# Context attention moved to other steps of an expert layer, two activations moved behind a copy, attention maxima taken negated

## The chip, the cores and the metric

One core of a Trainium2 chip runs the whole program. The metric is the device time in microseconds (us) of one execution, median over the runs. All arithmetic is in float32.

## What is computed

The reference has two blocks with a width of 1024 and a sequence of 256 tokens. Two parts of it matter here. The first is the mixture of experts that ends block one, the second is the attention of block two, on a context of 256 tokens (layer 0 only gives it an output) and on the latent tokens (both layers).

```python
# expert_choice_moe: 16 experts, each takes 32 of the 256 tokens
hid = jax.nn.silu(jnp.einsum('becd,edf->becf', xs, w_gate)) * jnp.einsum('becd,edf->becf', xs, w_up)
y = jnp.einsum('becf,efd->becd', hid, w_down) * g[..., None].astype(xn.dtype)

# block two, per head of 64
q_ga_c = rms_norm_2(to_heads(ga_qc, GQA_Q_HEADS), q_norm_w)
def context_attention(q, k, v):
    s = jnp.einsum('bgrqd,bgkd->bgrqk', q, k) * (q.shape[-1] ** -0.5)
    p = jax.nn.softmax(s, axis=-1).astype(v.dtype)
    return jnp.einsum('bgrqk,bgkd->bgrqd', p, v)

# layer 1 of the context only gives a state and keys
w = jnp.exp(b[:, :, -1:, :] - b)                 # key decays
return jnp.einsum('bhsd,bhsv->bhdv', k * w, v)
```

The context does not depend on block one, so its work can be done while block one still runs.

## The kernel before

Each engine runs one instruction list, in the order in which the program writes it, and waits on semaphores. All large weights come over SyncE's queue in one fixed order (`stream`) into a ring in SBUF of 4 x 4096 columns, that is four tiles of 2 MB (L3168 and L3166 issue them). A tile is issued when TensorE has finished with the tile whose place it takes (`freed`).

The mixture of experts is a list of 96 steps, `STEPS`: four groups of 16 steps "gate" and "up" (two halves for each of 4 experts) and 8 steps "down". Steps 16 to 23, 40 to 47, 64 to 71 and 88 to 95 are down steps. Every step reads two tiles of 2 MB: L1653 is the gate and up product (32 matmul records a tile), L1679 the down product (16 records a tile). At the head of a new expert, and of the first down step, TensorE turns the hidden tokens (L1667, `turn_hidden`), ScalarE copies them (L1916, `by_feature`), and the down product waits for that copy. After the last down step of a group VectorE copies the result out (L2273, L2274), and in the next four gate steps TensorE combines it into the tokens (L1692, `combine`) and VectorE adds it (L2251). In every second up step ScalarE takes the silu of the hidden values (L1912).

The context work is cut into 80 stages, `CTX_STAGES`, and `CTX_AT` says behind which step each stands. A stage is a piece of a generator on TensorE, ScalarE and VectorE alike (`context()`), run after the engine's own work of that step. Its weights, 0.5 to 1 MB, stand in the stream behind the step's tiles. The stages `lv0` to `lv2` (L844, with GpSimd's L3113 and VectorE's L2747 to L2754), `gla_out` (L863), `gla_norm` and `at0` to `at5` read no weights. Each of `at0` to `at5` does two heads: scores (L937), largest value (L2914, L2915), exponential (L2500), normalising (L2920, L2921), turning (L945), copy (L2301), values (L955), where one head's path goes over three engines.

Stage `gqa_kv1`, behind step 87, projects keys and values of context layer 1; ScalarE then evacuates them (L2301), squares the keys (L2360) and takes the key decays (L2386), all before it returns to the copy of step 88 (L1916).

The latent attention of each layer has 24 units of 128 queries and 512 keys. VectorE takes a unit's maximum (`largest`, L3012) and multiplies it by -1 or -0.125 (L3013), ScalarE uses it as the bias of the exponential (L2596), VectorE inverts the sum (L3018), GpSimd multiplies (L3123), TensorE turns.

## Time and profile before

| what | value |
|---|---|
| median of 3 runs | 2214.92 us (2212.74 to 2216.28) |
| the profiled execution's own time | 2211.93 us |
| its span | 2210.1 us |
| TensorE matmul busy | 1981.3 us, 90% |
| VectorE, ScalarE, GpSimd busy | 599.8, 423.2, 207.2 us |
| mean granted TensorE clock | 0.966 of full |
| HBM read | 661.08 MB |

The span begins with the first instruction. The expert steps fill about 301 to 1359 us of it, the latent layers what follows. A busy share is a mean over stages with different limits, and matmul busy time contains time in which the array ran at half clock, so 90% does not say that TensorE sets the time everywhere. The rows that a reader needs for each stage are in the section of rows below.

### The profile page before, as it was taken

The numbers are of one execution on the slowest core, as the hardware profiler recorded it, in microseconds if no ns is written. First come the engines' busy times: TensorE is split into PE (matmuls) and PEld (weight loads), VectorE is DVE, ScalarE is ACT, GpSimd is POOL, SyncE is SP. The second block draws the span as 40 slices with busy tenths as digits, with TensorE's granted clock in tenths as the row PEclk, the third lists the DMA queues.
The fourth block names the chain that finished last, engine by engine and source line by source line (L and its number), as shares of the span: only waits on it lengthen the run. The fifth ranks groups of instructions, "written<-read, shape, count | busy, mean of one in ns | idle before, by whom it ended". The sixth has DMA issues, their size and how long they took to land.

```text
span 2210.1 us, 32677 instructions
## 1 busy us (share of the span) xinstructions
PE 1981.3 (90%) x14122; PEld 1387.0 (63%) x14122; DVE 599.8 (27%) x1180; ACT 423.2 (19%) x778; POOL 207.2 (9%) x183
## 2 busy tenths in 40 slices
PE   8999898877888898887897887999999999999997
PEld 4857565633465466563574543856888877588886
DVE  6766300124402010000002003364432044640001
ACT  3122221221302000000002112444200032630001
POOL 0830000020000000000000000334000002700000
PEclk9999999978999999999999998999999999999999
DMA  9958999999999999999999998531686743044450
GB/s 366 369 228 356 364 422 423 417 424 424 376 427 424 426 425 425 423 423 425 425 424 426 422 376 331 136 115 39 217 295 202 179 143 116 1 153 152 129 157 20
DMA packets 181382, 664.24 MB, mean 301 GB/s; under 512 B 17431, under 2 KB 121400, under 8 KB 142648
## 3 DMA queue, kind: packets, MB, share of 16 engines
q1 hardware_dynamic: 181240, 662.15, 76.6%
q8 instruction: 112, 1.84, 0.3%
q14 instruction: 30, 0.25, 0.0%
HBM read 661.08 MB, written 1.05 MB: 300 GB/s over the span
## 4 chain that ended last, share of the span: by engine, by line
PE 48%; DMA 23%; ACT 3%; DVE 3%; issue 1%; ACTq 0%; POOL 0%; SPq 0%; DVEq 0%; POOLq 0%
PE ps L1203 19%; PE ps L682 10%; DMA ring<-in_w_gate 7%; DMA ring<-in_w_down_slots 7%; DMA ring<-in_context_weights 5%; PE ps L1653 4%; DMA ring<-in_w_up 4%; PE ps L1679 2%; PE ps L1038 2%; PE ps L1212 2%; PE ps L1002 2%; ACT arena L2596 1%; PE ps L844 1%; PE ps L708 1%; PE ps L1692 1%
## 5 line engine op out<-in xcount | busy, mean ns | idle before, releaser
L1203 PE MATMUL ps<-arena,ring 128*128 128x256 f32 x1984 | 429.9, 380 | 1.0 <-DVEq L391 0.9
L1203 PEld LDWEIGHTS ps<-arena,ring 128*128 128x128 f32 x1984 | 377.2, 190 | 53.6 <-issue 1.7
L1653 PE MATMUL ps<-ring,arena 128*32 128x256 f32 x4000 | 259.8, 406 | 81.0 <-DMA ring<-in_w_up 43.7
L682 PE MATMUL ps<-arena,ring 128*128 128x256 f32 (+1 forms) x1392 | 317.0, 388 | 8.4 <-DMA ring<-in_context_weights 8.3
L682 PEld LDWEIGHTS ps<-arena,ring 128*128 128x128 f32 (+1 forms) x1392 | 255.2, 189 | 76.0 <-DMA ring<-in_context_weights 25.7
L1653 PEld LDWEIGHTS ps<-ring,arena 128*32 128x32 f32 x4000 | 125.4, 115 | 200.4 <-DMA ring<-in_w_up 59.1
L2301 ACT ACTIVATE arena<-ps 128x512 f32<-128x512 f32 (+4 forms) x147 | 78.1, 531 | 754.9 <-PE ps L682 344.2
L1679 PE MATMUL ps<-ring,arena 128*32 128x512 f32 x1024 | 142.9, 686 | 60.1 <-DMA ring<-in_w_down_slots 53.2
L1679 PEld LDWEIGHTS ps<-ring,arena 128*32 128x32 f32 x1024 | 30.2, 119 | 153.4 <-DMA ring<-in_w_down_slots 88.4
L3113 POOL TENSOR_TENSOR XC<-XC,arena 128x256 f32<-128x256 f32 x32 | 23.4, 730 | 986.4 <-ACT XC L2395 966.2
L682 PE MATMUL ps<-ring,arena 128*128 128x256 f32 (+3 forms) x320 | 87.6, 425 | 0.0
L1294 PE MATMUL ps<-arena,ring 128*128 128x256 f32 x384 | 86.1, 386 | 1.4 <-ACTq L391 1.4
L3123 POOL TENSOR_SCALAR arena<-arena 128x512 f32<-128x512 f32 x48 | 78.5, 1635 | 88.2 <-DVE arena L3018 84.8
L2772 DVE SCALAR_TENSOR_TENSOR XC<-ps,arena,XC 128x256 f32<-128x256 f32 x48 | 23.2, 484 | 225.4 <-PE ps L1203 144.3
L1002 PE MATMUL ps<-arena,ring 128*128 128x256 f32 x352 | 78.6, 382 | 4.4 <-DMA ring<-in_context_weights 4.4
L1294 PEld LDWEIGHTS ps<-arena,ring 128*128 128x128 f32 x384 | 73.8, 193 | 13.0 <-DVEq L391 2.2
L1912 ACT ACTIVATE arena<-ps 128x256 f32<-128x256 f32 x32 | 12.3, 383 | 344.8 <-PE ps L1653 344.6
L1002 PEld LDWEIGHTS ps<-arena,ring 128*128 128x128 f32 x352 | 66.3, 190 | 19.0 <-DMA ring<-in_context_weights 8.9
L2266 DVE TENSOR_TENSOR arena<-arena,ps 128x256 f32<-128x256 f32 x32 | 13.5, 421 | 236.5 <-ACT arena L1912 235.5
L682 PEld LDWEIGHTS ps<-ring,arena 128*128 128x128 f32 x320 | 56.1, 190 | 27.1 <-issue 17.0
L3067 DVE TENSOR_TENSOR arena<-arena,ps 128x512 f32<-128x512 f32 x20 | 13.7, 687 | 210.6 <-PE ps L1203 210.6
L1038 PE MATMUL ps<-arena,ring 128*128 128x258 f32 x224 | 52.0, 384 | 0.8 <-ACT arena L2431 0.8
(389 smaller groups left out, 1977.8 us busy)
## 6 DMA issues: line engine op xcount, KB each, us to landing
ring<-in_w_down_slots SPq DMA_DIRECT2D x64, 2048.0 KB, 13.9
ring<-in_w_up SPq DMA_DIRECT2D x63, 2048.0 KB, 13.1
ring<-in_w_gate SPq DMA_DIRECT2D x62, 2048.0 KB, 13.5
ring<-in_w_ada SPq DMA_DIRECT2D x27, 2048.0 KB, 9.5
ring<-in_w_ffn_in SPq DMA_DIRECT2D x44, 1024.0 KB, 7.7
ring<-in_context_weights SPq DMA_DIRECT2D x35, 1024.0 KB, 13.4
ring<-in_w_ffn_out SPq DMA_DIRECT2D x16, 1408.0 KB, 7.3
ring<-in_w_in SPq DMA_DIRECT2D x9, 2048.0 KB, 11.2
```

The costliest lines, as they stand in the source:

```text
L682: m = mm(o, a, x, start=(k == 0 and r == 0), stop=(k == kt - 1 and last))
L1002: m = mm(b[i][:, T * x:T * x + T], w[:, k % 2, c:c + P], HID[:, k, :], start=(k == 0 and x == 0), stop=(k == 21 and x == 1))
L1038: m = mm(b[:, 0:RAW], w[:, k, c:c + P], raw[:, k, :], start=(k == 0), stop=(k == KD - 1))
L1203: m = mm(b, w[:, k, c:c + P], src[:, k, :], start=(k == 0), stop=(k == kt - 1))
L1212: m = mm(b[:, 0:T], held["w"][:, k, c:c + P], oT[X][:, k, :], start=(k == 0), stop=(k == KD - 1))
L1294: m = mm(b[:, T * i:T * i + T], w[:, k, P * (j + i):P * (j + i) + P], src(k), start=(k == 0), stop=(k == ktiles - 1))
L1653: m = mm(b[u][32 * c:32 * c + 32, T * x:T * x + T], xs[:, 2 * h + k, CAP * e:CAP * e + CAP], w[:, k, at_:at_ + T], start=(h == 0 and k == ...
L1679: m = mm(b[a][64 * n + 32 * j:64 * n + 32 * j + 32, :], hdT[:, 2 * a + j, ch, :], w[:, j, at_:at_ + W], start=(i == 0 and odd == 0), stop= ...
L2301: step(a(dst, src, f, **kw), frees=name if frees else None)
L2772: step(stt(out=x, in0=b[:, o:o + T], scalar=mod2[:, l, gate + m, st:st + 1], in1=x, op0=ALU.mult, op1=ALU.add), frees=name if last else None)
L3113: step(nc.gpsimd.tensor_tensor(hat[st][n % 2][:, x, :], ex[st][n % 2][:, x, :], glqk[:, x, :], ALU.mult), lev_ready if x else None)
L3123: step(nc.gpsimd.tensor_scalar(Pr[n % 8], Pr[n % 8], sm[:, n % 8:n % 8 + 1], None, ALU.mult), pn_ready[X])
```

## The change

Three edits. First, `CTX_AT` is written by `step_of`: every stage up to `at0` stands directly behind the one before (stage k at step k + 2), so that `na_v_a` to `gla_out` move one step ahead, `gla_norm` from step 23 to 21 and `at0` from 24 to 22. `at1` to `at4` move from steps 25, 26, 27, 28 to 23, 24, 26, 27; `at5` and `at_end` stay at 30 and 31, and all later stages stay. Second, in ScalarE's `context()` the squares and key decays of layer 1 stand behind `yield "gqa_kv1"`, so behind ScalarE's own work of step 88. Third, both `largest` take the maximum with its sign turned in one instruction, and the factor 0.125 of the "ga" heads moves into the root of the query norm: the root of (sum + 64 eps) is 8 times the root of (sum / 64 + eps).

```diff
--- before.py
+++ after.py
@@ -66,7 +66,7 @@
 
 TABLES1 = [("ident", 128), ("ones", 128), ("tri_f", 128), ("tri_b", 128), ("neg_f", 128), ("neg_b", 128),
            ("dft_c", 256), ("dft_s", 256), ("idft_c", 256), ("idft_s", 256), ("unused", 1056),
-           ("eps", 1), ("ln_eps", 1), ("pick", 8), ("token", 2), ("fold", 16)]
+           ("eps", 1), ("ln_eps", 1), ("pick", 8), ("token", 2), ("fold", 16), ("eps64", 1)]
 TABLES2 = [("half64", 128), ("flip64", 128), ("neg_col", 64), ("rope_c", 256), ("rope_s", 256),
            ("rope_r", 128), ("gla_lv", 160), ("diag32", 32), ("gla_bd", 256)]
 
@@ -102,6 +102,7 @@
     ang = 2 * np.pi * np.outer(half, by_parity(s)) / (2 * T)
     t["idft_c"], t["idft_s"] = np.cos(ang) / T, -np.sin(ang) / T
     t["eps"] = np.full((P, 1), EPS)
+    t["eps64"] = np.full((P, 1), 64 * EPS)
     t["ln_eps"] = np.full((P, 1), LN_EPS)
     t["unused"] = np.zeros((P, 1056))
     t["pick"] = (i[:, None] == 32 * (np.arange(8) // 2) + np.arange(8) % 2)
@@ -547,7 +548,16 @@
             STEPS += [("down", 8 * g + p) for p in range(8)]
 
         spread_over = len(STEPS) - 2
-        CTX_AT = {1 + k * (spread_over - 1) // len(CTX_STAGES) + (0 < k < 7): k for k in range(len(CTX_STAGES))}
+        heads = [name for name, _ in CTX_STAGES].index("at0")
+        between_combines = {heads + 1 + j: s for j, s in enumerate((23, 24, 26, 27, 30, 31))}
+
+        def step_of(k):
+            if k <= heads:
+                return k + 1 + (k > 0)
+            return between_combines.get(k, 1 + k * (spread_over - 1) // len(CTX_STAGES))
+
+        CTX_AT = {step_of(k): k for k in range(len(CTX_STAGES))}
+        assert list(CTX_AT) == sorted(CTX_AT)
         assert len(CTX_AT) == len(CTX_STAGES)
         for s, (kind, i) in enumerate(STEPS):
             if kind == "down":
@@ -2362,8 +2372,9 @@
             def head_roots(st, N, q):
                 c, n = ((0, 3), (3, 2))[q]
                 b = read_bank(act, f"gn{q}{N}")
+                scale, eps = (1.0, "eps64") if q == 0 else (1 / 64, "eps")
                 step(a(grow[st][0:64, c:c + n, :], b[0:64, 0:P * n].rearrange("p (c t) -> p c t", c=n), ACT.Sqrt,
-                       scale=1 / 64, bias=tb("eps")[0:64]), frees=f"gn{q}{N}")
+                       scale=scale, bias=tb(eps)[0:64]), frees=f"gn{q}{N}")
                 tell(gsqrt_ready[st])
 
             def na_q(N):
@@ -2493,11 +2504,10 @@
                 gla_roots(C, N)
 
                 def soft(n):
-                    kind, h = HEADS2[n]
                     act.wait_ge(nm_ready[C], n + 1)
                     b = read_bank(act, f"sc{n}{N}")
                     for e in range(2):
-                        step(a(Prc[:, n % 2, e, :], b[:, T * e:T * e + T], ACT.Exp, scale=1.0 if kind == "na" else 0.125,
+                        step(a(Prc[:, n % 2, e, :], b[:, T * e:T * e + T], ACT.Exp, scale=1.0,
                                bias=nmc[:, n % 2, e:e + 1], accum_out=smc[:, n % 2, e:e + 1]), frees=f"sc{n}{N}" if e else None)
                     tell(pe_ready[C])
 
@@ -2547,9 +2557,9 @@
                 yield "gqa_kv1_a"
                 gqa_k(C, 1, N)
                 gqa_v(C, 1, N)
+                yield "gqa_kv1"
                 gqa_k_squares(C, 1)
                 key_decays(1)
-                yield "gqa_kv1"
                 head_roots(C, N, 1)
                 yield "na_k1_a"
                 yield "na_k1"
@@ -2590,10 +2600,9 @@
                 gla_squares(X, 1 + l)
 
                 def soft(n):
-                    kind = UNITS2[n][0]
                     act.wait_ge(nm_ready[X], NU * l + n + 1)
                     b = read_bank(act, f"sc{n}{N}")
-                    step(a(Pr[n % 8], b[:], ACT.Exp, scale=1.0 if kind == "na" else 0.125,
+                    step(a(Pr[n % 8], b[:], ACT.Exp, scale=1.0,
                            bias=nm[:, n % 8:n % 8 + 1], accum_out=sm[:, n % 8:n % 8 + 1]), frees=f"sc{n}{N}")
                     tell(pe_ready[X])
 
@@ -2908,11 +2917,8 @@
                 yield "gla_out"
 
                 def largest(n):
-                    kind, h = HEADS2[n]
                     b = read_bank(dve, f"sc{n}{N}")
-                    m = nmc[:, n % 2, :]
-                    step(v.tensor_reduce(m, b[:].rearrange("p (e t) -> p e t", e=2), AX.X, ALU.max))
-                    step(ts(m, m, -1.0 if kind == "na" else -0.125, None, ALU.mult), nm_ready[C])
+                    step(v.tensor_reduce(nmc[:, n % 2, :], b[:].rearrange("p (e t) -> p e t", e=2), AX.X, ALU.max, negate=True), nm_ready[C])
 
                 def softmax(n):
                     dve.wait_ge(pe_ready[C], n + 1)
@@ -3006,11 +3012,8 @@
                     head_normed(X, l, N, q)
                 gla_out(X, N)
                 def largest(n):
-                    kind = UNITS2[n][0]
                     b = read_bank(dve, f"sc{n}{N}")
-                    m = nm[:, n % 8:n % 8 + 1]
-                    step(v.tensor_reduce(m, b[:], AX.X, ALU.max))
-                    step(ts(m, m, -1.0 if kind == "na" else -0.125, None, ALU.mult), nm_ready[X])
+                    step(v.tensor_reduce(nm[:, n % 8:n % 8 + 1], b[:], AX.X, ALU.max, negate=True), nm_ready[X])
 
                 def inverted(n):
                     dve.wait_ge(pe_ready[X], NU * l + n + 1)
```

Where the instructions stand. TensorE, from the end of `gla_out` in step 21 of the kernel before, on to the combine of step 25 (L1679 down, L1653 gate, L872 and L937 `gla_norm`, L937/L945/L955 attention, L1692 combine):

```order
L1679 MATMUL ps<-ring,arena 32x512 x32
L872 MATMUL ps<-arena 128x512
L937 MATMUL ps<-arena 128x256 x2
L1653 MATMUL ps<-ring,arena 32x256 x32
L1692 MATMUL ps<-arena 128x256 x2
L937 MATMUL ps<-arena 128x256 x2
L945 MATMUL ps<-tab,arena 128x128 x4
L937 MATMUL ps<-arena 128x256 x2
L945 MATMUL ps<-tab,arena 128x128 x4
L955 MATMUL ps<-arena 64x256 x2
L1653 MATMUL ps<-ring,arena 32x256 x32
L1692 MATMUL ps<-arena 128x256 x2
```

and TensorE at the same place of the changed kernel, where lines stand 9 or 10 further down (L1689 down, L947/L955/L965 attention):

```order
L1689 MATMUL ps<-ring,arena 32x512 x16
L882 MATMUL ps<-arena 128x512
L947 MATMUL ps<-arena 128x256 x2
L1689 MATMUL ps<-ring,arena 32x512 x16
L947 MATMUL ps<-arena 128x256 x2
L955 MATMUL ps<-tab,arena 128x128 x4
L947 MATMUL ps<-arena 128x256 x2
L955 MATMUL ps<-tab,arena 128x128 x4
L965 MATMUL ps<-arena 64x256 x2
L1689 MATMUL ps<-ring,arena 32x512 x16
L947 MATMUL ps<-arena 128x256 x2
L955 MATMUL ps<-tab,arena 128x128 x4
```

`gla_norm` (L882, then L947) now stands before steps 22 and 23, and the first two heads between the down products of steps 22 and 23, where two down steps used to follow each other.

ScalarE, from the silu of step 87 to the root of the key norms, of the kernel before (L2301 evacuations, L2360 square, L2386 key decays, L1916 copy of turned tokens, L2365 root):

```order
L1912 ACT_TABLE_LOAD
L1912 ACTIVATE arena<-ps 128x256 x2
L2301 ACTIVATE arena<-ps 128x2x256
L2301 ACTIVATE arena<-ps 128x256
L2360 ACTIVATE arena<-arena 128x512
L2386 ACT_TABLE_LOAD
L2386 ACTIVATE arena<-arena 128x256 x2
L1916 ACTIVATE arena<-ps 128x512
L2365 ACT_TABLE_LOAD
L2365 ACTIVATE arena<-ps,tab 64x256
```

and of the changed kernel (L1926 is the copy, L2370 the square, L2397 the decays):

```order
L1922 ACT_TABLE_LOAD
L1922 ACTIVATE arena<-ps 128x256 x2
L2311 ACTIVATE arena<-ps 128x2x256
L2311 ACTIVATE arena<-ps 128x256
L1926 ACTIVATE arena<-ps 128x512
L2370 ACTIVATE arena<-arena 128x512
L2397 ACT_TABLE_LOAD
L2397 ACTIVATE arena<-arena 128x256 x2
L2376 ACT_TABLE_LOAD
L2376 ACTIVATE arena<-ps,tab 64x256
```

The copy moved ahead of one square, one table load and two exponentials.

VectorE, the first maxima of a latent layer, of the kernel before (L3012 maximum, L3013 factor, L3018 inverse of a sum):

```order
L3012 TENSOR_REDUCE arena<-ps 128x1
L3013 TENSOR_SCALAR arena<-arena 128x1
L3012 TENSOR_REDUCE arena<-ps 128x1
L3013 TENSOR_SCALAR arena<-arena 128x1
L3012 TENSOR_REDUCE arena<-ps 128x1
L3013 TENSOR_SCALAR arena<-arena 128x1
L3018 RECIPROCAL arena<-arena 128x1
L3012 TENSOR_REDUCE arena<-ps 128x1
```

and of the changed kernel (L3016 maximum, L3021 inverse):

```order
L3016 TENSOR_REDUCE arena<-ps 128x1 x3
L3021 RECIPROCAL arena<-arena 128x1
L3016 TENSOR_REDUCE arena<-ps 128x1
L3021 RECIPROCAL arena<-arena 128x1
```

The factor behind each maximum is gone.

## Rows read from the trace of the kernel before

**Rows 1.** The page: rate over 40 slices of 55.3 us, and the chain by engine.

```profile
GB/s 366 369 228 356 364 422 423 417 424 424 376 427 424 426 425 425 423 423 425 425 424 426 422 376 331 136 115 39 217 295 202 179 143 116 1 153 152 129 157 20
...
PE 48%; DMA 23%; ACT 3%; DVE 3%; issue 1%; ACTq 0%; POOL 0%; SPq 0%; DVEq 0%; POOLq 0%
```

**Rows 2.** Busy time by stretch; last three columns TensorE clock, DMA share, GB/s.

```profile
560.00:570.00 10.00, 9.36 (x104) 5.32 (x100) 3.94 (x9) 3.75 (x12) 0.00 (x0) 1.00 0.94 375
570.00:580.00 10.00, 7.15 (x65) 4.10 (x58) 4.71 (x11) 5.16 (x10) 0.00 (x0) 0.94 0.98 387
580.00:590.00 10.00, 8.97 (x86) 5.08 (x85) 2.88 (x6) 2.12 (x6) 0.00 (x0) 0.89 0.79 300
590.00:600.00 10.00, 9.55 (x109) 5.42 (x112) 3.75 (x10) 3.45 (x10) 0.00 (x0) 1.00 0.93 360
```

**Rows 3.** Timeline of TensorE, 478 to 620 us: start, us, what, [idle before].

```profile
478.90 0.75 PE L844 MATMUL ps<-arena 32*32 32x32 f32 x64 [1.51 <-POOL arena L3113]
...
504.78 2.19 PE L1679 MATMUL ps<-ring,arena 128*32 128x512 f32 x16 [2.06 <-DMA ring<-in_w_down_slots]
510.27 3.59 PE L863 MATMUL ps<-arena 128*64 128x256 f32 x16 [3.31 <-DVEq L391]
...
534.30 3.62 PE L1653 MATMUL ps<-ring,arena 128*32 128x256 f32 x32 [2.42 <-DMA ring<-in_w_gate]
...
546.89 4.18 PE L1653 MATMUL ps<-ring,arena 128*32 128x256 f32 x64
...
559.00 3.66 PE L1653 MATMUL ps<-ring,arena 128*32 128x256 f32 x64
...
568.60 3.66 PE L1653 MATMUL ps<-ring,arena 128*32 128x256 f32 x64
...
582.56 3.66 PE L1653 MATMUL ps<-ring,arena 128*32 128x256 f32 x64
...
594.14 3.66 PE L1653 MATMUL ps<-ring,arena 128*32 128x256 f32 x64
...
619.61 1.02 PE L1653 MATMUL ps<-ring,arena 128*32 128x256 f32 x5 [2.87 <-DMA ring<-in_w_gate]
```

**Rows 4.** Timeline of SyncE's DMA issues, 560 to 600 us.

```profile
561.00 11.65 SPq L3168 DMA_DIRECT2D ring<-in_w_gate  x4
584.56 13.64 SPq L3168 DMA_DIRECT2D ring<-in_w_up  x4
```

**Rows 5.** Timeline of VectorE, copy of the down product.

```profile
527.99 0.68 DVE L2273 COPY arena<-ps 64x512 f32<-64x512 f32 x1 [4.28 <-PE ps L1679]
```

**Rows 6.** Timeline of TensorE, 1261 to 1304 us.

```profile
1261.76 3.42 PE L1653 MATMUL ps<-ring,arena 128*32 128x256 f32 x32 [2.36 <-DMA ring<-in_w_up]
...
1276.28 6.39 PE L1679 MATMUL ps<-ring,arena 128*32 128x512 f32 x32 [3.93 <-ACTq L391]
...
1288.40 3.64 PE L1679 MATMUL ps<-ring,arena 128*32 128x512 f32 x32
...
1303.40 1.92 PE L1679 MATMUL ps<-ring,arena 128*32 128x512 f32 x16 [2.99 <-DMA ring<-in_w_down_slots]
```

**Rows 7.** Timeline of ScalarE, 1271 to 1276 us.

```profile
1271.97 0.38 ACT L2301 ACTIVATE arena<-ps 128x256 f32<-128x256 f32 x1 [1.39 <-PE ps L682]
...
1273.03 1.28 ACT L2386 ACT_TABLE_LOAD   x1
...
1275.49 0.60 ACT L1916 ACTIVATE arena<-ps 128x512 f32<-128x512 f32 x1
```

**Rows 8.** Groups by line between 1462 and 1528 us: count | busy, mean ns.

```profile
L3012 DVE TENSOR_REDUCE arena<-ps 128x1 f32<-128x512 f32 x24 | 16.6, 691 | 4.9 <-PE ps L1139 3.7 <-DVE arena L3013 0.3
...
L3013 DVE TENSOR_SCALAR arena<-arena 128x1 f32<-128x1 f32 x24 | 3.7, 153 | 0.8
```

**Rows 9.** Chain that ended last, L3013's first and last of 12 rows.

```profile
1464.10 0.16 DVE arena L3013
...
1921.46 0.16 DVE arena L3013
```

## The prediction

> **What bounds the kernel now.** I read the page first. The chain by engine gives TensorE 48% and DMA 23%, so two things take turns. The rate over 40 slices says where: from slice 6 to 23 (276 to 1271 us) it stands at 417 to 427 GB/s except in slice 11 (376), and slice 24 falls to 376 [rows 1]. Where the rate is flat the expert steps wait for weights, and work moved there is worth nothing. The dips are time in which the queue had nothing to fetch, and since the steps behind them are again paced by DMA, each byte not fetched there comes late at the end.
>
> The windows place the first dip at 560 to 600 us, with 375, 387, 300 and 360 GB/s, while the TensorE clock stayed at 0.89 to 1.00 [rows 2]. How long it is, I take from the timeline of TensorE. A row that was ended by DMA tells when a tile landed. From 504.78 to 534.30 six tiles landed, 4.92 us each. Step 24's second tile landed at 534.30, and step 32's second at 619.61: 85.3 us for 16 tiles, with no context weights between, where 16 x 4.92 is 78.7 [rows 3]. **6.6 us are lost**. The windows agree: 1422 of 4 x 425 is 6.5 us missing.
>
> Why: five attention stages follow each other behind steps 24 to 28, and a step's experts (3.66) plus its stage take longer than the 9.84 us in which DMA brings two tiles. From the starts of the expert rows, a stage with a combine and added tokens takes 559.00 - 551.07 = 7.9 us, one without 568.60 - 562.66 = 5.9, one beside a silu and a turn 582.56 - 572.26 = 10.3 [rows 3]. TensorE falls behind. I call lag the time from a step's first tile landing (534.30 + 4.92, then each 9.84) to its being used up (start + 1.83): step 26 landed 549.1, used 560.8, lag 11.7; step 27 11.5; step 28 15.6. The next issues behind the one at 561.00 wait for those, and the queue has an issue only at 584.56 when the last tile landed at about 583.7 [rows 4]. Lags of 11.5 and more cost bytes here. The three other tiles in the ring are worth 3 x 4.92 = 14.8 us, so from a lag of 14.8 on the queue stands empty in any case; between the two it is a matter of how a transfer begins and ends.
>
> The second dip. Step 87's second tile landed at 1261.76, step 90's second at 1303.40, 41.64 us [rows 6]. In it came the two tiles each of steps 88, 89 and 90 (6 x 4.92 = 29.5 us) and 0.5 + 0.75 + 0.75 MB of context weights (4.9 us by bytes), 34.4 together. **7.2 us are lost**. TensorE idled 3.93 us before step 88 at 1276.28 for ScalarE, and then ran 32 matmuls in 6.39 us, where the same 32 took 3.64 at full clock one step later [rows 6]. ScalarE was free at 1272.35, spent until 1275.49 on a square, a table load and two exponentials, and only then copied the tokens (0.60) that the down product waits for [rows 7].
>
> In the latent layers no DMA holds anything, and the chain passes from ScalarE to VectorE and back: L3013, the factor on the maximum, stands in it 12 times [rows 9].
>
> **The change part by part.**
>
> *Attention stages.* Work and bytes stay, the place changes. I walk the new order with the durations above. Stages up to `gla_out` come one step earlier; their own waits for GpSimd (1.51 before the third level) and VectorE (3.31 before `gla_out`) come with them [rows 3] and stand in steps where the lag is near zero (504.78 and 534.30 both waited for DMA). Step 22's second tile lands at 514.6 and is used at 516.5. `at0`, 5.9, to 522.4. Step 23's second tile lands at 524.5, used 526.4. Here VectorE first copies the down product, two copies of 0.68 for the second half [rows 5], 1.4 before `at1` can normalise: 5.9 + 1.4, to 533.7. Step 24 to 537.4, combine and `at2` 7.9, to 545.3. Step 25: first tile landed 539.2, used 547.1, lag 7.9, all done at 549.0, combine about 2, to 551. Step 26 to 555.9, `at3` 5.9, to 561.8. Step 27 to 565.7, `at4` with silu and turn 10.3, to 576.0. Step 28: landed 568.8, used 577.9, **lag 9.1, the largest**. Two steps without a stage bring it to 4.9 and then none. 9.1 is under 11.5, so nothing is lost: the term is 6.6 at most, and I take 6.3, since the margin to the smallest lag seen to cost is 2.4 us. The bound from below is a loss like that of 570 to 580 and 590 to 600, 0.9 + 1.5 for two steps near the edge, and half as much again: 2 to 3 us gained.
>
> *Copy before decays.* The copy starts when the turn is there, near 1272.4, and ends at 1273.05: step 88 starts 3.2 us sooner (1276.28 - 1273.1). The decays are needed only two steps later by the keys' turn, and the square by the head sums behind `na_k1_a`, after step 88. With 0.8 instead of 3.93 us idle the product may run at full clock, 6.39 - 3.64 = 2.75 less. Bounds: 3.1 (copy alone) and 7.2 (all that is lost). I take 4.5, the wait and half of the clock.
>
> On the table load a row and a page differ. The load took 1.28 us from 1273.03, and the interval from 1272.35 to the copy's start at 1275.49 is 3.14 in all [rows 7]. The Trainium skill, "ScalarE: Activation LUTs", section "What ACT_TABLE_LOAD costs", puts a drain of about 1.38 us on top of the load for every switch of set. By the rows the wait removed is 3.2 us, by the page it would be an estimated 4.6. That interval holds the switch whole, drain or none, so the rows decide.
>
> *Maxima.* A maximum took 0.69 us and its factor 0.153 [rows 8], 0.18 to 0.19 from start to next start. No row has a maximum with its sign turned. Its bounds are the plain one (0.69) and maximum plus factor (0.87), which would make the edit worth nothing; input, output and form are the plain one's, so I take 0.69. It counts only where VectorE is in the chain, 12 x 0.185 = **2.2 us**; elsewhere ScalarE's exponentials cover it. Bounds 0 and 3. In the context stages 12 such factors fall from each head's path, which only widens the margin above. The factor 0.125 in the root and the wider table cost no instruction.
>
> **Sum.** 6.3 + 4.5 + 2.2 = 13.0 us. The profiled execution took 2211.93, which gives 2198.9. It lies 3.0 under the median of 2214.92 and below its lowest, so against the median I say 2214.9 - 13.0 = **2201.9, 2202 us**. Range of this case 2198 to 2206.
>
> **Rivals.**
>
> *The ring still runs dry, 17%.* Down steps 22 and 23 are worse hosts than I reckon (levels, `gla_norm` with its long reciprocal, and copies pile up before `at0`). For: slack ahead of `at0` is one step less than before. Against: both steps around it waited for DMA. Price: of 6.6 only 0 to 3 come back, so 2205 to 2208.
>
> *The tail's loss moves, 10%.* The two exponentials now stand before the root of the key norms, and the next release is behind `na_k1_a` in any case, so only part of 3.1 shows in landings. Price 3 us, 2205.
>
> *Negation isn't free or is hidden, 6%.* A gain of 2.2 less: 2204.
>
> *The tail returns all of its loss, 4%.* 7.2 for 4.5: 2199.
>
> *Half clock in the attention steps, slower, 3%.* Mechanism: with less backlog TensorE stops more often for tiles and heads, and its clock falls to 1.2 GHz from step 22 to 30. A tile of experts then takes 3.62 us, as the one at 534.30 did, where the tiles of the step at 559.00 took 1.83 [rows 3], so a step costs 3.6 more, the stages' own matmuls not counted. The margin is 14.8 - 9.1 = 5.7; to eat the whole gain and 4.4 more takes (13.0 + 4.4 + 5.7) / 3.6, seven of the nine steps, and from there it ends slower: with all nine, 2202 + 9 x 3.6 - 5.7 = 2229. For: the slow tiles at 534.30 and at 1261.76 stand right behind waits of 2.4 us [rows 3, 6]. Against: in 560 to 600, with waits of about 1 us inside the stages, the clock stood at 0.89 to 1.00 [rows 2]. The Trainium skill, "TensorE: Matmul & The Clock Gate", section "HAM oscillation — how this bites in real kernels", says that short bursts between waits for DMA can leave the array at half rate at every tile. By that page the edit would lose what this rival prices; the rows of the dense stages speak for full clock.
>
> **How the numbers follow.** The forecast has 60%. The range takes the case's own bounds and the first three rivals: low 2215 - (6.6 + 7.2 + 3) = 2198, high 2215 - (2 + 3.1 + 0.5) = 2209. 0.2% (4.4 us) is about what a measurement of this kernel can tell from no change; all but the worst mixes of the first rivals stay beyond it. Faster 0.88, same 0.09, slower 0.03.
>
> **What the changed profile would show.** No window under 415 GB/s between 500 and 650 us, and step 32's second tile at about 613. Step 88's down product less than 1 us after the turn, with 32 matmuls in under 5 us, and the last down tile some 11 us earlier than 1356. In the latent layers maxima of 0.69 us in a row and each layer about 1 us shorter. Wrong would be: an expert row in steps 24 to 30 that starts more than 11 us behind its tile, a new wait before step 88, or a negated maximum of 0.85 us.

## The result and the profile after

The changed kernel takes 2200.52 us (median of 5 runs, 2196.05 to 2205.09), the kernel before, beside it, 2214.56 (2212.42 to 2216.28). The ratio is 0.9943 [0.9928, 0.9959], 12.6 us less; in a later comparison on its own it was 0.9955 [0.9941, 0.9968], 10.0 us less. 2202 us was forecast. The runs of the changed kernel spread over 9 us, those of the kernel before over 4, and the profiled execution of the changed one is the slowest of its five, 2205.09.

The page has its rates over 40 slices and the chain by engine, which answer to [rows 1]:

```profile
GB/s 365 372 199 343 339 420 424 417 427 426 421 426 427 423 418 426 420 425 426 421 425 426 416 423 343 140 116 39 222 294 199 180 144 116 1 153 153 129 158 20
...
PE 58%; DMA 30%; DVE 5%; ACT 4%; issue 1%; POOL 1%; SPq 1%; ACTq 0%; DVEq 0%; POOLq 0%
```

The dip in slice 11 (376) is gone, it reads 421; slice 24 reads 423 where it was 376, and slice 23 in front of it 416. Slices 3 and 5 are lower than before, and no edit stands there.

Windows of the changed kernel (last three columns TensorE clock, DMA share, GB/s), which answer to [rows 2]:

```profile
540.00:550.00 10.00, 10.00 (x83) 5.30 (x82) 2.41 (x6) 1.73 (x5) 0.00 (x0) 0.75 1.00 423
550.00:560.00 10.00, 8.51 (x87) 4.61 (x87) 4.40 (x9) 3.46 (x10) 0.00 (x0) 1.00 1.00 406
560.00:570.00 10.00, 9.54 (x92) 5.56 (x91) 4.50 (x9) 2.30 (x8) 0.00 (x0) 1.00 0.98 415
...
580.00:590.00 10.00, 8.85 (x112) 5.03 (x112) 2.86 (x6) 2.82 (x7) 0.00 (x0) 1.00 1.01 428
```

Of the 6.5 us of bytes that were missing between 560 and 600, some 0.7 are left, (425 - 406 + 425 - 415) / 42.5, and they stand behind a stretch with the clock at 0.75. The timeline of TensorE in the changed kernel says how far behind it was (L1663 gate and up, L1689 down):

```profile
522.93 1.92 PE L1689 MATMUL ps<-ring,arena 128*32 128x512 f32 x16 [2.97 <-DMA ring<-in_w_down_slots]
...
532.72 1.92 PE L1689 MATMUL ps<-ring,arena 128*32 128x512 f32 x16 [0.19 <-DMA ring<-in_w_down_slots]
...
544.23 4.05 PE L1663 MATMUL ps<-ring,arena 128*32 128x256 f32 x64
...
556.21 3.66 PE L1663 MATMUL ps<-ring,arena 128*32 128x256 f32 x64
...
583.14 3.66 PE L1663 MATMUL ps<-ring,arena 128*32 128x256 f32 x64
...
623.01 2.29 PE L1663 MATMUL ps<-ring,arena 128*32 128x256 f32 x24 [2.65 <-DMA ring<-in_w_gate]
```

From step 22's second tile (522.93) to step 32's (623.01) are 100.1 us for 20 tiles of 4.92, 98.4: 1.7 us lost. Some 0.4 of it were lost when step 27's second tile landed (572.51), and 1.2 between 602.14 and 623.01, where the windows miss no bytes (428, 418 and 436 GB/s); the count by landings and the bytes of the windows agree to about 1 us. Step 25 (556.21) has the largest lag: its first tile landed at 532.72 + 3 x 4.92 = 547.5 and was used up at 558.0, 10.5. Step 28's is 8.0. The lag here is the prediction's, from the landing of a step's first tile to the moment when it is used up.

At step 88 the timelines of TensorE and ScalarE answer to [rows 6, 7] (L2311 projection, L1926 copy, L2370 square, L2397 decays):

```profile
1264.85 3.27 PE L1663 MATMUL ps<-ring,arena 128*32 128x256 f32 x32 [3.13 <-DMA ring<-in_w_up]
...
1276.49 3.64 PE L1689 MATMUL ps<-ring,arena 128*32 128x512 f32 x32 [0.88 <-ACTq L392]
...
1300.43 1.92 PE L1689 MATMUL ps<-ring,arena 128*32 128x512 f32 x16 [2.94 <-DMA ring<-in_w_down_slots]
```

```profile
1275.22 0.38 ACT L2311 ACTIVATE arena<-ps 128x256 f32<-128x256 f32 x1 [1.38 <-PE ps L692]
1275.70 0.60 ACT L1926 ACTIVATE arena<-ps 128x512 f32<-128x512 f32 x1
1276.42 0.63 ACT L2370 ACTIVATE arena<-arena 128x512 f32<-128x512 f32 x1
1277.06 1.28 ACT L2397 ACT_TABLE_LOAD   x1
1278.36 1.05 ACT L2397 ACTIVATE arena<-arena 128x256 f32<-128x256 f32 x2
```

TensorE idles 0.88 us instead of 3.93 and the product runs in 3.64 instead of 6.39, and from step 87's second tile to step 90's are 35.6 us instead of 41.6. The groups by line of VectorE (1456 to 1520 us) have the maximum alone, with the duration of [rows 8]:

```profile
L3016 DVE TENSOR_REDUCE arena<-ps 128x1 f32<-128x512 f32 x24 | 16.6, 692 | 3.7 <-PE ps L1149 2.8
```

Where the time went, by stretches between the starts of the same instructions (the first silu of an expert group's step, VectorE's copy of a group's result, the first and last exponential of a latent layer). "Again" is the same kernel profiled once more, in a later run; every stretch is worked out from the starts in the timelines, the first from silus at 309.74, 314.07, 318.16 and 308.86:

| stretch, us | before | before again | changed | changed again |
|---|---|---|---|---|
| start to silu, step 3 | 309.7 | 314.1 | 318.2 | 308.9 |
| to copy, step 23 | 218.3 | 217.2 | 216.6 | 217.8 |
| to silu, step 51 | 317.9 | 316.7 | 314.1 | 312.7 |
| to silu, step 87 | 419.2 | 419.2 | 419.0 | 418.8 |
| to copy, step 95 | 94.2 | 92.7 | 88.2 | 89.6 |
| to first exponential | 106.3 | 105.1 | 106.5 | 106.3 |
| latent layer 0, first to last | 47.8 | 47.8 | 45.3 | 45.2 |
| to layer 1 | 367.3 | 367.3 | 367.2 | 367.1 |
| layer 1, first to last | 45.3 | 45.3 | 44.0 | 43.9 |
| to the end | 284.1 | 284.1 | 284.1 | 284.1 |
| span | 2210.1 | 2209.4 | 2203.0 | 2194.5 |

The first stretch has the same instructions in all four, and it moves by 9 us. The first profile of the changed kernel got 8.4 us more there than the first profile of before, which hides more than half of what the edits gave behind it.

### The profile page after: what moved, and what is told of

It is laid out like the page before. It is cut to its first block, busy times and chain, and to the rows that moved or that the text cites. A ratio compares the mean times of both kernels' runs of the same rounds, so it can differ in the third digit from the quotient of the medians.

```text
span 2203.0 us, 32618 instructions
## 1 busy us (share of the span) xinstructions
PE 1987.3 (90%) x14122; PEld 1389.8 (63%) x14122; DVE 588.5 (27%) x1120; ACT 423.4 (19%) x778; POOL 206.2 (9%) x183
## 4 chain that ended last, share of the span: by engine, by line
PE 58%; DMA 30%; DVE 5%; ACT 4%; issue 1%; POOL 1%; SPq 1%; ACTq 0%; DVEq 0%; POOLq 0%
PE ps L1213 19%; PE ps L692 11%; DMA ring<-in_w_up 8%; DMA ring<-in_w_gate 7%; DMA ring<-in_w_down_slots 7%; DMA ring<-in_context_weights 6%; PE ps L1663 5%; PE ps L1689 2%; PE ps L1048 2%; PE ps L1012 2%; PE ps L1323 2%; DMA arena<-in_w_ada 2%; PE ps L1222 2%; PE ps L1568 1%; ACT arena L2605 1%
## 5 line engine op out<-in xcount | busy, mean ns | idle before, releaser
L1663 PE MATMUL ps<-ring,arena 128*32 128x256 f32 x4000 | 260.5, 407 | 76.2 <-DMA ring<-in_w_up 43.4
L1663 PEld LDWEIGHTS ps<-ring,arena 128*32 128x32 f32 x4000 | 125.4, 115 | 194.9 <-DMA ring<-in_w_up 59.4
L2311 ACT ACTIVATE arena<-ps 128x512 f32<-128x512 f32 (+4 forms) x147 | 78.2, 532 | 739.7 <-PE ps L692 326.8
L1689 PE MATMUL ps<-ring,arena 128*32 128x512 f32 x1024 | 136.9, 660 | 54.4 <-DMA ring<-in_w_down_slots 50.6
L1689 PEld LDWEIGHTS ps<-ring,arena 128*32 128x32 f32 x1024 | 29.0, 114 | 141.1 <-DMA ring<-in_w_down_slots 87.0
L692 PE MATMUL ps<-ring,arena 128*128 128x256 f32 (+3 forms) x320 | 87.6, 425 | 0.0
L1304 PEld LDWEIGHTS ps<-arena,ring 128*128 128x128 f32 x384 | 72.5, 190 | 12.6 <-DVEq L392 2.2
## 6 DMA issues: line engine op xcount, KB each, us to landing
ring<-in_w_in SPq DMA_DIRECT2D x9, 2048.0 KB, 11.6
```

Of the source, the lines that this page charges most:

```text
L692: m = mm(o, a, x, start=(k == 0 and r == 0), stop=(k == kt - 1 and last))
L1304: m = mm(b[:, T * i:T * i + T], w[:, k, P * (j + i):P * (j + i) + P], src(k), start=(k == 0), stop=(k == ktiles - 1))
L1663: m = mm(b[u][32 * c:32 * c + 32, T * x:T * x + T], xs[:, 2 * h + k, CAP * e:CAP * e + CAP], w[:, k, at_:at_ + T], start=(h == 0 and k == ...
L1689: m = mm(b[a][64 * n + 32 * j:64 * n + 32 * j + 32, :], hdT[:, 2 * a + j, ch, :], w[:, j, at_:at_ + W], start=(i == 0 and odd == 0), stop= ...
L2311: step(a(dst, src, f, **kw), frees=name if frees else None)
```

## The experiments

Two theories stood for the attention stages. **Lag**: bytes are lost when the largest lag of a step passes a bound between 9 and 11.5 us. **Gap**: any step without a stage between the attention stages is enough, whatever the lag. The intervals below are 95% ones, and the us beside them are the ratio times the time of the kernel before. For the other two edits: each gives its term by itself, against the rivals on record.

**The three edits, each alone.** The diffs are the parts of the change: `CTX_AT` alone; `yield "gqa_kv1"` alone; the negated maxima with the root's scale alone.

> The kernel before with the first edit alone, the stages' places. Theory of the lag in the ring: all of the 6.6 us lost between step 24 and 32 come back, so 6.3 us less (5 to 6.6, ratio 0.997), and from step 24's to step 32's second tile 78.7 instead of 85.3 us, while the second dip at step 88 stays as it was, 41.6 us from step 87's to step 90's second tile. Rival (the stages' own waits of three engines travel with them and the queue runs dry elsewhere): 0 to 3 us less, and windows under 415 GB/s between 500 and 600 us.

> The kernel before with the second edit alone, squares and key decays of layer 1 behind the copy. Theory: step 88 starts 3.2 us sooner and its 32 matmuls take less than 5 us, 4.5 us less in all (3.1 to 7.2, ratio 0.998), 37 instead of 41.6 us from step 87's to step 90's second tile; 560 to 600 us stays at 1422 of 1700. Rival (the next release is paced by the stage behind, so the loss only moves): under 1.5 us less.

> The kernel before with the third edit alone, maxima negated and the factor in the query root. Theory: a negated maximum takes 0.69 us like the plain one, 2.2 us less in the two latent layers (12 places of 0.185), and in the context heads each turn comes 0.19 us sooner, which takes 2 us off the lag at step 28 and so brings back 1 to 2 of the 6.6 us there: 3 to 4 us less, ratio 0.9985. Rival (ScalarE covers it): under 1 us less, latent attention as long as before, 64 us and 62 us windows with the same chain.

Measured, against a kernel before at 2211.83: stages alone 2209.06, 0.9987 [0.9976, 0.9998], 2.9 us; copy alone 2207.94, 0.9977 [0.9968, 0.9986], 5.1 us; maxima alone 2209.41, 0.9988 [0.9976, 0.9999], 2.7 us. The sum is 10.7, where the whole change gave 10.0 and 12.6: the edits add up, and none takes from another beyond the noise, which is some 2 us for each.

For the stages alone the expected 5 to 6.6 us did not come: 2.9 lies in the rival's 0 to 3. The rows are nearer to the theory: no window between 500 and 600 us is under 415 GB/s, and from step 22's second tile (519.17) to step 32's (618.56) 1.0 us is lost. The maxima's trace loses 4.4 us between step 24's and step 32's second tiles (543.09 to 626.19), not clearly less than other traces of the old order (4.6 to 6.6), so the 1 to 2 us that were expected there are not shown.

In the copy's trace ScalarE's copy follows the projection directly and TensorE's rows at step 88 are those of the changed kernel:

```profile
1263.98 3.26 PE L1653 MATMUL ps<-ring,arena 128*32 128x256 f32 x32 [2.26 <-DMA ring<-in_w_up]
...
1275.29 3.64 PE L1679 MATMUL ps<-ring,arena 128*32 128x512 f32 x32 [0.88 <-ACTq L391]
...
1298.76 1.92 PE L1679 MATMUL ps<-ring,arena 128*32 128x512 f32 x16 [2.49 <-DMA ring<-in_w_down_slots]
```

34.8 us from tile to tile; 34.4 is all that the bytes need. In the trace with the stages alone the same stretch takes 40.5 (1260.48 to 1300.97), so the gain there is the copy's alone.

**A denser placement.** The changed kernel with `at1` to `at4` behind steps 23 to 26:

```diff
-between_combines = {heads + 1 + j: s for j, s in enumerate((23, 24, 26, 27, 30, 31))}
+between_combines = {heads + 1 + j: s for j, s in enumerate((23, 24, 25, 26, 30, 31))}
```

> The changed kernel with at1 to at4 behind steps 23, 24, 25, 26 instead of 23, 24, 26, 27, so that five attention stages again follow each other and two meet a combine. Theory of the lag: what counts is how far TensorE is behind when its tiles land. By the same walk the largest lag is 9.6 us at step 26 (landed 549.1, used 558.7, times of the first trace), under the 11.5 that cost bytes, so the time is that of the changed kernel, within 1 us. Rival (the gaps between the heads and the free combines made the gain): the queue runs dry again and 3 to 6 us are lost.

Measured 2203.15, 0.9954 [0.994, 0.9969]; the time can't tell it from the changed kernel. Its windows can:

```profile
550.00:560.00 10.00, 8.57 (x87) 5.08 (x88) 3.96 (x8) 2.22 (x7) 0.00 (x0) 1.00 0.97 382
560.00:570.00 10.00, 9.55 (x92) 5.28 (x91) 3.95 (x9) 3.81 (x12) 0.00 (x0) 1.00 0.92 364
570.00:580.00 10.00, 8.39 (x108) 4.83 (x111) 3.23 (x7) 5.26 (x12) 0.00 (x0) 1.00 0.98 404
```

2.9 us of bytes are missing. The lags, from its rows as above, are 11.2, 13.0 and 12.6 for steps 25, 26 and 27. So lags above 11 cost bytes, as lag says. But the expectation's walk failed, which had 9.6 and no loss: the clock was at 0.71 from 520 to 530, and step 23's 32 matmuls took 5.10 us (527.94 to 533.04) instead of 3.64.

Half clock does the same to the places of the change. The norm-first kernel further down has them unaltered, and its trace shows

```profile
540.00:550.00 10.00, 10.00 (x83) 5.39 (x83) 2.62 (x7) 1.73 (x5) 0.00 (x0) 0.76 0.91 356
550.00:560.00 10.00, 8.51 (x87) 4.62 (x87) 4.40 (x9) 3.46 (x10) 0.00 (x0) 1.00 0.96 377
560.00:570.00 10.00, 9.54 (x92) 5.56 (x91) 4.49 (x9) 2.30 (x8) 0.00 (x0) 1.00 0.97 411
```

That is 3.1 us of bytes missing (2.1 by landings, 520.19 to 620.71), with lags of 11.4 and 13.2 at steps 24 and 25. So the dense trace shows what a lag costs, and not that the denser places are the worse ones.

**One stage moved in the kernel before.** Only `at4` goes from step 28 to 29, and in a second kernel only `at5` from step 30 to 29, so that six stages stand in a row:

```diff
+CTX_AT[29] = CTX_AT.pop(28)
```

```diff
+CTX_AT[29] = CTX_AT.pop(30)
+CTX_AT = dict(sorted(CTX_AT.items()))
```

> The kernel before with one stage moved alone, at4 from step 28 to 29. Theory of the lag: step 28 still begins at 582.6, 15.6 us behind its tile, and its four rows before stay, so the 300 GB/s of 580 to 590 us stay; step 29 begins at about 588, lag 11.5 instead of 17.4, and 590 to 600 us goes from 360 to about 420. 1 to 2 us less in all, 84 instead of 85.3 us from step 24's to step 32's second tile. Rival (five stages without a gap are what costs, so any gap heals it): 80 us and 5 us less.

> The kernel before with one stage moved alone, at5 from step 30 to 29, so that six attention stages follow each other. Theory of the lag: step 29 is already 17.4 us late, and with a stage behind it step 30 starts 7 us later than before, at about 606, so the queue stands empty again: 600 to 610 us falls from 424 to about 360 GB/s and 3 to 5 us more are lost, 89 instead of 85.3 us from step 24's to step 32's second tile. Rival (the loss is only that of whatever follows step 27's silu): no change.

The first measured 2211.22 beside 2212.83, 0.9989 [0.9976, 1.0001]. The interval is 2.4 us less, from 5.3 less to 0.2 more, so the time does not show a gain. Its loss between step 24's and step 32's second tiles (534.32 to 614.58) is 1.5 us, and only one window shows it, behind step 28 with a lag of 12.5:

```profile
570.00:580.00 10.00, 7.16 (x52) 4.12 (x48) 5.12 (x12) 5.27 (x13) 0.00 (x0) 1.00 1.00 421
580.00:590.00 10.00, 9.88 (x136) 5.60 (x128) 1.97 (x5) 0.60 (x1) 0.00 (x0) 1.00 0.94 370
```

The second measured 2214.3 beside 2211.94, 1.0016 [1.0003, 1.0029], 3.5 us slower (0.7 to 6.4). Its windows, behind 382 and 406 GB/s from 560 to 580:

```profile
580.00:590.00 10.00, 8.48 (x81) 4.88 (x82) 2.17 (x6) 3.35 (x9) 0.00 (x0) 0.83 0.80 300
590.00:600.00 10.00, 8.51 (x86) 4.87 (x87) 5.21 (x12) 3.46 (x10) 0.00 (x0) 1.00 1.01 394
600.00:610.00 10.00, 7.45 (x64) 4.18 (x60) 4.38 (x10) 3.61 (x7) 0.00 (x0) 1.00 0.91 387
610.00:620.00 10.00, 8.12 (x132) 4.75 (x124) 1.27 (x3) 1.37 (x3) 0.00 (x0) 1.00 0.91 349
```

8.0 us are lost (537.12 to 623.86 for 16 tiles) where before lost 6.6; the time is as expected, the 86.7 us from tile to tile less than the 89. Its lags at steps 26, 27 and 28 are 11.6, 11.3 and 15.4, those of before, but the missing bytes go on to 620, where the kernel before has no stage at step 29 and catches up. So one stage more behind a lag costs. That one less gives back is not settled. The 80.3 us of the at4 kernel are the number of the gap rival (80), where lag had 84, but part of them is the clock's: steps 26 and 27, ahead of the stage that moved, ended 10.1 and 9.8 us behind their tiles, in the first trace of before 11.8 and 11.5. The two traces of the old order that have 10.1 and 9.8 or 9.9 there as well, the unchanged kernel again and the copy alone, lost 4.6 and 5.0. So the single gap may be worth about 3 us in the rows, and it leaves as little lost as the whole first edit; the lag of 12.5 at step 28 still cost its window.

**The unchanged kernel and the changed kernel once more.**

> The kernel before, unchanged, one more trace. In the changed kernel's trace the stretch up to the first silu of the experts took 318.2 us, in the one of before 309.7, though no instruction in it changed. If that is the spread of a stretch from run to run, this trace differs from 309.7 by several us as well and the later stretches (218, 318, 419, 94, 106, 48, 367, 45, 284 us) agree within 1 us. If the wider table or the changed order made it longer, it is 309 to 311 again.

> The changed kernel again, for its spread. If the first stretch (to the first silu of the experts) is what varies, its time here is 2196 to 2205 with a ratio of 0.994 to the kernel before, and the later stretches agree with the first trace's within 2 us.

The unchanged kernel took 2211.29 in its one execution; it loses 4.6 us in the attention steps (538.44 to 621.77), not 6.6, and takes 41.3 us from step 87's tile (1263.81) to step 90's (1305.13). The changed kernel took 2200.79, 0.9955 [0.9941, 0.9968], as expected. The later stretches agree with the first trace of each within 1.5 us; for the unchanged kernel 1 us had been expected, and four of them differ by 1.1 to 1.5. The first stretch differs by 4.3 and 9.3 us. The changed kernel's TensorE timeline is the cleanest view of the walk:

```profile
513.65 3.58 PE L1689 MATMUL ps<-ring,arena 128*32 128x512 f32 x16 [2.44 <-DMA ring<-in_w_down_slots]
...
522.98 3.64 PE L1689 MATMUL ps<-ring,arena 128*32 128x512 f32 x32
...
533.97 3.66 PE L1663 MATMUL ps<-ring,arena 128*32 128x256 f32 x64
...
545.56 3.66 PE L1663 MATMUL ps<-ring,arena 128*32 128x256 f32 x64
...
553.18 1.93 PE L1663 MATMUL ps<-ring,arena 128*32 128x256 f32 x32 [1.04 <-DMA ring<-in_w_up]
...
575.06 3.66 PE L1663 MATMUL ps<-ring,arena 128*32 128x256 f32 x64
```

and its window where `at1` ran:

```profile
530.00:540.00 10.00, 9.29 (x88) 5.15 (x86) 3.52 (x8) 3.35 (x10) 0.00 (x0) 1.00 1.01 428
540.00:550.00 10.00, 8.76 (x88) 5.09 (x88) 3.78 (x8) 3.45 (x10) 0.00 (x0) 1.00 1.01 426
```

Step 23 to step 24 is `at1`: 533.97 - 522.98 - 3.64 = 7.35 us, where the walk has 5.9 + 1.4 = 7.3. Step 28's tile landed at 553.18 + 3 x 4.92 = 567.9 and was used at 576.9, lag 9.0, where the walk has 9.1. No window from 530 to 620 is under 421. In the first profile the same stage took 544.23 - 532.72 - 1.92 = 9.6, with the clock at 0.75 in its window. Part of the stage ran at half rate in one execution (four matmuls of L947 took 2.07 us at 539.29, and 1.13 at 534.57) and all of it at full rate in the other, with one program.

**Beyond the change.** After the third edit the latent round is still tied to VectorE: the reciprocal of a norm stands between the unit maxima. The chain of the changed kernel through one round (L2605 exponential, L2311 copy, L3021 inverse, L3052 norm reciprocal, L3016 maximum):

```profile
1483.94 0.79 ACT arena L2605 x2
...
1484.86 0.17 DVE arena L3021
1485.06 1.77 DVE arena L3052
...
1486.85 0.70 DVE arena L3016
...
1487.58 0.79 ACT arena L2605 x2
```

The first of two further kernels puts that reciprocal, and the products of the norm, ahead of the last two inverses of a round, for which VectorE had waited 1.51 us. The second also takes the next round's first maximum ahead of the last inverse.

```diff
-                    if n < NU:
-                        inverted(n + 2)
-                        inverted(n + 3)
-                    if j == 0:
-                        rotated(0)
-                        rotated(1)
                     ...
                     if j == 4:
                         ...
                         tell(o_ready)
+                    if n < NU:
+                        inverted(n + 2)
+                        inverted(n + 3)
+                    if j == 0:
+                        rotated(0)
+                        rotated(1)
```

> The changed kernel with VectorE's work on the norm of the linear attention (two reciprocals of 1.75 us, a product pair of 1.77 us) and the last rotation put ahead of the inverses of units 2 and 3 of their group, where VectorE idles about 1.5 us for ScalarE, instead of behind them, where the next maximum and so ScalarE wait. In a latent layer of the kernel before the chain goes ScalarE, inverse, this work, maximum, ScalarE. Theory (the latent attention is paced by that round, not by ScalarE alone or GpSimd): each of four groups is about 1.5 us shorter, first to last exponential of a layer 45.3 and 44.0 us go to about 39.5 and 38, 11 us less in all, ratio 0.995 to the changed kernel and 0.989 to the kernel before. Rival (GpSimd's four products of 1.63 us a group, now fed later, become the bound): 2 to 5 us less.

> The kernel of e6 with each group's first maximum taken ahead of the inverse of the last unit before it, so that ScalarE need not wait for VectorE at a group's edge. Theory: the edge costs ScalarE another 1.0 us (inverse 0.17 and maximum 0.69 and what lies between) at five edges a layer, until GpSimd's 6.5 us a group set the pace; 38 goes to about 35, 5 to 8 us less than e6, 16 to 19 less than the changed kernel's 2200. Rival (TensorE and GpSimd are the bound already in e6): the same as e6 within 2 us.

The first measured 2192.44, 0.9905 [0.9886, 0.9924] against before, some 8 us below the changed kernel's 2200.5 (which ran beside other runs of before), and is the fastest. 11 us had been expected. The second measured 2195.2, 0.9919 [0.9901, 0.9938]: nothing on top, where 5 to 8 us had been expected. In the first the layers take 41.6 and 39.9 us from first to last exponential, 3.7 and 4.1 less than the changed kernel; 39.5 and 38 had been expected. In the second they take 43.1 and 40.7, 1.5 and 0.8 more than in the first. One round takes 6.7 us (1478.05 to 1484.75) where it took 7.9 (1487.58 to 1495.51). The chain says what now bounds it:

```profile
1478.05 2.11 PE ps L1142 x8
1480.16 0.60 PE ps L1155 x4
1480.77 0.02 issue
1480.79 0.61 ACT arena L2311
1481.40 0.14 issue
1481.53 0.63 PE ps L1155 x4
1482.16 0.09 issue
1482.25 0.63 PE ps L1155 x4
1482.88 1.88 PE ps L1166 x16
1484.75 2.11 PE ps L1142 x8
```

It is TensorE with a single ScalarE copy between the turns. VectorE has left the chain, so an earlier maximum, as in the second, has nothing there to shorten. GpSimd is close behind: its four products of a round take 6.53 us from 1480.74, and it idles 0.17 before the next, so the rival that names GpSimd is not excluded as the next bound. Why the second kernel's layers are longer was not tried.

## Why the prediction was right, and where its sizes were off

**The whole.** 13.0 us were summed, 12.6 and 10.0 were measured. The forecast case is the one that came about; no rival did as a whole, though part of the first is in it. That the first comparison came within 0.4 us of the sum is luck: the edits alone add up to 10.7, and the rows below to 10.2 (3.9, 4.1 and 2.2). Luck is also in the time: 2202 was reckoned from 2214.9, a median of three, where the kernel before had 2211.83, 2212.83 and 2211.94 in the later comparisons (29, 17 and 13 runs).

**Attention stages, 6.3 us summed, 2.9 [0.4, 5.3] measured: the mechanism right, the size off.** The step of the prediction that failed is "6.6 us are lost", taken as a property of the kernel. It was that of one execution: the unchanged kernel lost 4.6 in another, 5.0 in the trace of the copy alone (537.99 to 621.70) and 4.4 in that of the maxima. The second is "9.1 is under 11.5, so nothing is lost": in the five traces with the new places 1.7 (changed), 0.7 (changed again), 1.0 (stages alone), 2.1 (norm-first kernel) and 0.8 (the one after it) are still lost by landings. The means are 5.2 and 1.3, 3.9 less. The walk's durations hold where the clock is full: from step to step, 23 to 28, the changed kernel again has 11.0, 11.6, 4.7, 10.7 and 14.2 us, the walk 11.3, 11.6, 5.7, 10.8 and 14.2; only the combine behind step 25 was put too long, 2 us for 1. What it left out is half clock, and so "step 25, lag 7.9" failed, with 10.5 in the first profile, 2.3 of the 2.6 more from `at1` partly at half clock, and with 9.0 in the other, where step 22's second tile (513.65) took 3.58 us instead of 1.92 ahead of `at0`. "9.1, the largest" was 10.5 and 9.0. What the runs put in place of 6.3 is 3.9: the stretch from the silu of step 3 to that of step 51 takes 534.8 us in the four traces of the old places (before, before again, copy alone, maxima alone; 533.9 to 536.2) and 531.0 in the five of the new (530.1 to 531.9). From step 23's copy on it is 4.4 (317.5 to 313.1), but that copy itself comes later in the new order, which has two heads in front of it. "Lags of 11.5 and more cost bytes here" stands: 11.2 to 13.0 cost 2.9 us, 11.4 and 13.2 cost 3.1, 10.5 cost 0.7, 9.0 cost nothing. Its sign of being wrong, a row that starts more than 11 us behind its tile, appeared once, in the norm-first kernel: step 25 started at 556.21, 11.4 behind 544.8. The first rival's price (0 to 3 us back) holds by time and its mechanism in part: in all five traces step 22's second tile was still waited for, so nothing had piled up ahead of `at0`, but in three of them that tile then took 3.0 to 3.6 us instead of 1.92.

**Copy before decays, 4.5 us summed, 5.1 [3.1, 7.1] measured: right.** The wait fell by 3.05 us and the product's clock came back whole, 2.75, not half. In the rows this is 6.0 us from tile to tile, and 1.2 are still missing of 7.2. Less than 6.0 arrives later: the stretch from step 87's silu to step 95's copy is 3.1 to 6.0 us shorter in the pairs of the table, and over all traces 4.1: 93.0 (six with the copy late; 91.1 to 94.3) to 88.9 (six with it early; 87.6 to 90.5). Where the other 1.9 go is open; the dense kernel's trace, with the copy early, took 37.0 us from tile to tile (1260.76 to 1297.79). The rival in which the tail's loss moves is refuted at step 88 by the copy's own trace, 34.8 us of 34.4; those rows speak for the rival that the tail returns all of its loss, and what arrives speaks for the 4.5.

The table load and its page: the load took 1.28 us from 1277.06 and the exponentials start at 1278.36, 0.02 behind it; the removed interval was 3.05 us by TensorE's idle time. The Trainium skill, "ScalarE: Activation LUTs", section "What ACT_TABLE_LOAD costs", has 1.28 us for the load, which agrees, and a drain of about 1.38 on top, which no row here shows as time of its own. By rows the term was 3.2, by the page 4.6; the rows were right.

**Maxima, 2.2 us summed, 2.7 [0.2, 5.3] measured: right.** The negated maximum takes 0.692 us, the plain one 0.691. With the edit alone layer 1 went from 45.26 to 43.87 us, 1.39 for the 7 places of the chain that fall in it at 0.185 (1.30), and layer 0 from 47.75 to 46.89, 0.86 for five (0.93). The changed kernel's 2.5 in layer 0 is not all the edit's: the chain of before has TensorE's L1132 at 2.00 us for four matmuls at 1473.98, where four take 1.06 at full clock later on, and the changed kernel has 1.06 throughout; with the maxima alone 2.01 stands there still. The dense kernel has all three edits and took 46.86 in layer 0, with 2.01 at that place. So the 1.6 us come from where the clock happened to be.

**The profile that was promised.** Three readings failed as stated: the 415 GB/s floor (406 at 550 to 560) and step 32's second tile at about 613, which landed at 623.01 because the span up to the first silu was 8.4 us longer; counted from step 22's second tile it is as forecast to 1.7 us. The third: the last down tile came at 1353.13 and not 11 us but 3.1 us earlier than 1356.27, with the same 8.4 in between; in the second profile it came at 1344.13, 12.1 earlier. The order at step 88, 0.88 us and 32 matmuls in 3.64, and 0.69 us for each maximum came as said.

**Half clock.** The slower case did not come about. In the first profile the clock fell in a stretch of one stage (0.75) and in the steps that wait for DMA, and stood at 1.00 from 550 to 590. The Trainium skill, "TensorE: Matmul & The Clock Gate", section "HAM oscillation — how this bites in real kernels", has short bursts between waits for DMA at half rate; where steps wait for a tile (592.35, 602.14 in the changed kernel: 3.19 and 2.75 us for 32 matmuls instead of 1.93) the trace agrees, but not at every tile: the one at 522.93, behind a wait of 2.97 us, took 1.92. A slow tile between two waits cost nothing there, since the next one hadn't landed.

**Open.** Why one and the same program takes from 308.9 to 318.2 us to its first silu was not tried. And what a lag near 10 us costs isn't settled by its size alone: at 10.1 and 9.8 the windows of the at4 kernel read 426 and 421 GB/s, those of the unchanged kernel again 403 and 405, those of the copy alone 408 and 398. How a transfer loses bytes while other tiles are still in the ring was only argued.

## What to carry to other kernels

Walk the lag, not the idle time: for a ring of buffers, add up how far behind its tile each step ends, in the new order, from durations of rows; the walk's steps were met to 0.3 us but for one, where the clock was full. One stage moved out of the worst step may have given about as much as the twelve that the first edit moved, though its time (2.4 us, 5.3 less to 0.2 more) doesn't prove it. But take what is lost now from more than one execution, since the half-clock stretches move, and one trace may show the worst case; and leave the walk a margin of one stage at half clock, which was 2.3 us here. When an engine copies something that another waits for, let nothing stand ahead of it that is needed only later, in particular nothing that loads a table.

## What the runs showed that was not expected

- The same instructions, from the start to the first expert silu, took 308.9, 309.7, 314.1 and 318.2 us in four executions of two kernels. Over all twelve traces the stretch goes with the clock from 250 to 300 us: 308.9 and 309.7 at 0.97, 311.0 to 312.9 at 0.93, 313.2 to 315.4 at 0.90, 318.2 and 318.4 at 0.85. The traces with the wider table span 308.9 to 318.4, those without it 309.7 to 314.1, so the table isn't shown to lengthen it. What moves the clock is open. A single trace is no measure for a change under 9 us.
- Three other tiles in the ring are 14.8 us of cover by count, but lags of 11.2 to 13.0 already cost 2.9 us in three windows.
- The places of the change are not safe in every execution: with one stage at half clock the same order lost 3.1 us of bytes in one trace and none in another.
- A reciprocal of 128x256 took 1.75 us on VectorE (L3052) and held the latent round; moved by a few lines it gave 8 us, over half of what the three edits had given.
